# Mixer A's gate products on rounded high and low parts, in the middle of a projection step

## The chip, the cores and the metric

The kernel runs on one core of one Trainium2 chip. The time is the device time of one execution in microseconds (us); of repeated executions the median is taken. TensorE (PE) multiplies, VectorE (DVE), ScalarE (ACT) and GpSimd (POOL) work on vectors, SyncE (SP) and POOL issue the DMAs. Each engine works through its own list of instructions in order and waits for the others at semaphores.

## The reference, cut to what matters

The reference is one step of a one-layer hybrid decoder: 2048 prompt tokens and 8 x 4 sample tokens, width 1024. One input projection gives nine groups of 256 columns; four token mixers (A to D) share them; then come an output projection, a layer norm and a squared-ReLU MLP with a second norm. The change is in mixer A, whose gates `r` and `i` are 64 x 64 products per head:

```python
    xc, new_buf_a = causal_conv(xa, buf_a, conv_a_w)      # width 4, depthwise
    xc = xc + conv_a_b
    # rglru(xc, ...):
    xh = xc.reshape(B, T, N_HEADS, HEAD_DIM)              # 4 heads of 64
    r = jax.nn.sigmoid(jnp.einsum('bthi,hij->bthj', xh, wa).reshape(B, T, W_GROUP) + ba)
    i = jax.nn.sigmoid(jnp.einsum('bthi,hij->bthj', xh, wx).reshape(B, T, W_GROUP) + bx)
    log_a = -RGLRU_C * r * jax.nn.softplus(-lam)
    a = jnp.exp(log_a)
    b = jnp.sqrt(-jnp.expm1(2.0 * log_a)) * (i * xc)
    # h_t = a_t * h_(t-1) + b_t over the tokens
    ya = ha * jax.nn.gelu(ga)
```

## The kernel before, in words

Everything is kept channels first: 128 channels on the partitions, tokens along the row. The 2080 tokens are cut into five blocks of 416 (`BLK`). A product that needs more precision than one rounded (`fp32r`) product gives is made of three: weights and input are each split into a rounded high part (ACT copies to `fp32r`) and the rest (DVE subtracts), and high x high, high x low and low x high are summed in PSUM.

The input projection runs in 88 steps (`P_STEPS`, counted by `j`). A step is one tile of 128 output columns for one block: 24 rounded products (`project`, L869 to L871), into one of three PSUM banks in turn. ACT copies the result out (`put_out`, L1306), and SP stores it to a scratch in DRAM. A step can start only when the result three steps before it has been copied out. Steps 0 to 19 make the four tiles that mixer A needs, block by block; from step 20 on the order is tile by tile, and the mixers run beside the projection.

Mixer A has ten passes, n = 0 to 9: two halves of 128 channels (two heads each) times five blocks. Where the work of a pass stands is set by a table: `A_AT` gives pass n to step 21 + 3n. In the lists of the engines that means:

- POOL loads the pass's two inputs from the scratch (`a_load`), after it has stored the result of the pass two before (`put`, L2482) and that store has ended, since the buffers are shared.
- DVE: `a_conv(n)` makes the convolution (L1802, L1804) at step 21 + 3n, then `a_rest(n - 1)` finishes the pass before: five operations, L1834 to L1849, the scan over the tokens among them.
- PE: `a_gates(n)` (L903) stands ahead of the next step, 22 + 3n: two plain f32 products of `gsel` (for each half of the channels a 128 x 128 matrix with the two heads' 64 x 64 gates on its diagonal) with `a_conv`, into the banks PS 6 and PS 7.
- ACT: `a_act(n)` (L1336) follows `put_out` of step 21 + 3n: two sigmoids out of PSUM (L1343, L1345), then exp, tanh, square root and gelu, with four table loads between them.

The fifth block (n = 4 and 9) holds the sample tokens too, so its convolution and its scan are made of more instructions. Mixer B (`b_mix`, at the steps of `B_AT`, from 37 on) and mixer D (`D_AT`, from 50 on; it uses a third matrix in `gsel`) follow in the same lists.

A table `SPLIT` says at which step the next weight tile is split: ACT's `split_hi` (L1271) stands behind `put_out` of that step, DVE's `split_lo` (L1687) one step later, and waits for it. The entries between steps 21 and 50 are 24, 29, 34, 39, 44 and 49. DVE's place for a step has this order: `a_conv`, `a_rest`, `b_mix`, `d_mix`, `split_lo`.

Before step 20 SP loads the gates into `gsel` with 12 DMAs (L565), and DVE and ACT make the constants of the recurrence (`lam`) from `lru_lambda`.

Of the kernel before, what the change touches and what calls it, by code (L numbers as in the profile page):

```python
# [81 lines left out]
CONST_ALL = 16 * 18  # L82
# [165 lines left out]
def build(nc, x_all, w_all, pvec, lnp, rows2, gates_a, gates_x, poolw, sbh, sbr, masks, ident_d, ck, cv, ptab,  # L248
          st_h, st_a, st_b, st_p, y_out, kv_out, so_out):
    ctx = ExitStack()  # L250
    with ctx:
# [42 lines left out]
        with ExitStack() as e1:  # L294
# [7 lines left out]
            with ExitStack() as f:  # L302
# [14 lines left out]
                d1 = sb("d_sum_a", [P, LASTW + BUFP + DECB * (BUFP + DECT)], F32, f)  # L317
                d2 = sb("d_sum_b", [P, LASTW + BUFP + DECB * (BUFP + DECT)], F32, f)
                d5 = sb("d_mean", [P, BLK], F32, f)
                d6 = sb("d_out", [P, BLK], F32, f)  # L320
# [133 lines left out]
        s_mzero = sem("gate_weights_zeroed")  # L454
        s_axc, s_agp, s_agev, s_aact, s_amade = sem("a_conv_made"), sem("a_gates_done"), sem("a_gates_evacuated"), sem("a_act_done"), sem("ya_made")
# [105 lines left out]
        def _(sp):  # L561
# [71 lines left out]
            for c in range(2):  # L633
                for n, src in enumerate((gates_a, gates_x, poolw)):
                    for h in range(2):
                        const(gsel[HD * h:HD * h + HD, c, n, HD * h:HD * h + HD], src[2 * c + h])
# [201 lines left out]
        def _(pe):  # L838
# [12 lines left out]
            def project(j, amid=(), turned=()):  # L851
# [363 lines left out]
            for j in range(NB * GRP, N_P):  # L1215
                if j - 1 in A_AT:
                    a_gates(A_AT[j - 1])
# [7 lines left out]
                project(j, p_taus(j, 1))  # L1225
# [35 lines left out]
        def _(act):  # L1261
# [75 lines left out]
            def a_act(n):  # L1337
# [13 lines left out]
                act.activation(ag[:, n % 2, :], ag[:, n % 2, :], ACT.Gelu_apprx_tanh).then_inc(s_aact, 1)  # L1351

# [1246 lines left out]
```

## Time and profile before

| | |
|---|---|
| median of 3 runs | 2453.49 us (2453.25 to 2456.35) |
| the profiled execution | 2453.47 us |
| its span, first to last instruction | 2451.9 us |
| PE busy | 2410.5 us, 98% |
| DVE busy | 1587.5 us, 65% |
| ACT busy | 1287.9 us, 53% |
| mean granted clock of TensorE | 0.997 |

The span is what the rows count in; 1.6 us of the profiled execution's time lie around it. In a group of instructions, "idle before" is how long the engine stood still just ahead of them, and the name behind the arrow is what ended that. In a timeline a row is a stretch of equal instructions with its start and its length; matmuls overlap, so the spacing of their starts is what one costs. A table load stands as a row of its own on ACT.

### The profile page before, as it was taken

The numbers are of one execution on the slowest core, as the hardware profiler recorded it, in microseconds if no ns is written. First come the engines' busy times: TensorE is split into PE (matmuls) and PEld (weight loads), VectorE is DVE, ScalarE is ACT, GpSimd is POOL, SyncE is SP. The second block draws the span as 40 slices with busy tenths as digits, with TensorE's granted clock in tenths as the row PEclk, the third lists the DMA queues.
The fourth block names the chain that finished last, engine by engine and source line by source line (L and its number), as shares of the span: only waits on it lengthen the run. The fifth ranks groups of instructions, "written<-read, shape, count | busy, mean of one in ns | idle before, by whom it ended". The sixth has DMA issues, their size and how long they took to land.

```text
span 2451.9 us, 36722 instructions
## 1 busy us (share of the span) xinstructions
PE 2410.5 (98%) x13263; PEld 2330.7 (95%) x13263; DVE 1587.5 (65%) x2234; ACT 1287.9 (53%) x1981; POOL 242.4 (10%) x526
## 2 busy tenths in 40 slices
PE   7999999999999999999999999999999999999998
PEld 7999999999999999999999999999999999999998
DVE  7535662656777787777778777757755665863335
ACT  5466523545656745556555566554445555444432
POOL 0011320200101100111100011000122130000000
PEclk9999999999999999999999999999999999999999
DMA  8434554533444434444443443433566674343332
GB/s 256 152 110 140 165 170 131 168 120 127 160 126 157 130 117 140 131 149 141 122 131 124 130 146 115 133 115 117 173 192 183 203 238 140 117 136 120 112 115 86
DMA packets 141526, 351.64 MB, mean 143 GB/s; under 512 B 20625, under 2 KB 64146, under 8 KB 141218
## 3 DMA queue, kind: packets, MB, share of 16 engines
q1 hardware_dynamic: 128994, 312.88, 40.2%
q0 software_dynamic: 12352, 36.42, 4.7%
q8 instruction: 106, 1.74, 0.3%
q14 instruction: 74, 0.61, 0.1%
HBM read 300.11 MB, written 49.12 MB: 142 GB/s over the span
## 4 chain that ended last, share of the span: by engine, by line
PE 92%; DVE 3%; ACT 2%; issue 1%; DMA 1%; SPq 0%; DVEq 0%; ACTq 0%
PE PS L1133 21%; PE PS L1135 21%; PE PS L1134 21%; PE PS L871 5%; PE PS L869 5%; PE PS L870 5%; PE PS L939 2%; PE PS L961 1%; PE PS L960 1%; PE PS L929 1%; PE PS L1023 1%; PE PS L930 1%; PE PS L1053 1%; PE PS L1011 1%; PE PS L909 1%
## 5 line engine op out<-in xcount | busy, mean ns | idle before, releaser
L1433 ACT ACTIVATE w_hi_lo<-w_raw 128x1024 fp32r<-128x1024 f32 x240 | 253.0, 1054 | 282.8 <-PE PS L1135 276.7
L1133 PE MATMUL PS<-a_hi,w_hi_lo 128*128 128x416 f32 x1080 | 385.0, 356 | 1.9 <-DVE a_lo L2185 1.9
L1135 PE MATMUL PS<-a_hi,w_hi_lo 128*128 128x416 f32 x1080 | 378.9, 351 | 0.0
L1134 PE MATMUL PS<-a_lo,w_hi_lo 128*128 128x416 f32 x1080 | 378.1, 350 | 0.0
L1986 DVE TENSOR_TENSOR w_hi_lo<-w_raw,w_hi_lo 128x1024 fp32r<-128x1024 f32 x240 | 292.7, 1220 | 57.2 <-ACT w_hi_lo L1433 54.9
L1133 PE MATMUL PS<-h_hi,w_hi_lo 128*128 128x416 f32 x824 | 294.3, 357 | 0.0
L1135 PE MATMUL PS<-h_hi,w_hi_lo 128*128 128x416 f32 x824 | 289.8, 352 | 0.0
L1134 PE MATMUL PS<-h_lo,w_hi_lo 128*128 128x416 f32 x824 | 288.9, 351 | 0.0
L2013 DVE TENSOR_TENSOR h_lo<-h_full,h_hi 128x416 fp32r<-128x416 f32 x160 | 94.6, 592 | 224.1 <-ACT h_hi L1448 223.9
L1133 PEld LDWEIGHTS PS<-a_hi,w_hi_lo 128*128 128x128 f32 x1080 | 202.8, 188 | 5.4 <-DVE a_lo L2185 2.8
L1134 PEld LDWEIGHTS PS<-a_lo,w_hi_lo 128*128 128x128 f32 x1080 | 203.3, 188 | 2.1
L1135 PEld LDWEIGHTS PS<-a_hi,w_hi_lo 128*128 128x128 f32 x1080 | 202.4, 187 | 2.3
L1433 ACT ACTIVATE w_hi_lo_c<-w_raw 128x1024 fp32r<-128x1024 f32 x120 | 126.5, 1054 | 132.8 <-PE PS L1135 128.4
L1444 ACT ACTIVATE h_full<-PS 128x416 f32<-128x416 f32 x160 | 82.5, 516 | 200.6 <-PE PS L1135 198.8
L1133 PE MATMUL PS<-a_hi,w_hi_lo_c 128*128 128x416 f32 x520 | 185.2, 356 | 2.2 <-DVE a_lo L2019 2.0
L1942 DVE TENSOR_TENSOR_SCAN n_prompt<-n_prompt 128x512 f32<-128x512 f32 (+3 forms) x160 | 178.9, 1118 | 8.6 <-POOL n_prompt L2508 8.4
L1135 PE MATMUL PS<-a_hi,w_hi_lo_c 128*128 128x416 f32 x520 | 183.2, 352 | 0.0
L1134 PE MATMUL PS<-a_lo,w_hi_lo_c 128*128 128x416 f32 x520 | 182.5, 351 | 0.0
L1986 DVE TENSOR_TENSOR w_hi_lo_c<-w_raw,w_hi_lo_c 128x1024 fp32r<-128x1024 f32 x120 | 146.3, 1220 | 34.1 <-ACT w_hi_lo_c L1433 33.2
L1134 PEld LDWEIGHTS PS<-h_lo,w_hi_lo 128*128 128x128 f32 x824 | 155.6, 189 | 2.1
L1133 PEld LDWEIGHTS PS<-h_hi,w_hi_lo 128*128 128x128 f32 x824 | 155.3, 188 | 2.2 <-issue 0.4
L1135 PEld LDWEIGHTS PS<-h_hi,w_hi_lo 128*128 128x128 f32 x824 | 154.8, 188 | 1.6
(334 smaller groups left out, 5206.4 us busy)
## 6 DMA issues: line engine op xcount, KB each, us to landing
w_raw<-w_all SPq DMA_DIRECT2D x380, 512.0 KB, 3.5
proj_scratch<-stage SPq DMA_DIRECT2D x70, 208.0 KB, 2.0
k_rows<-kv_out SPq DMA_DIRECT2D x80, 128.0 KB, 4.1
v_hi_lo<-v_scratch SPq DMA_DIRECT2D x40, 256.0 KB, 4.3
x_scratch<-x_full SPq DMA_DIRECT2D x20, 416.0 KB, 2.7
x_residual<-x_scratch SPq DMA_DIRECT2D x5, 1664.0 KB, 7.8
pages<-ck SPq DMA_DIRECT2D x64, 128.0 KB, 2.2
pages<-ck POOLq DMA_DIRECT2D x64, 128.0 KB, 2.6
```

Source lines behind the costliest of these rows:

```text
L869: pe.matmul(out, w_h, x_hi(b)[:, k, :], start=(k == 0), stop=False)
L870: pe.matmul(out, w_h, x_lo(b)[:, k, :], start=False, stop=False)
L871: ins = pe.matmul(out, w_l, x_hi(b)[:, k, :], start=False, stop=(k == KT - 1))
L939: ins = pe.transpose(PS[:, 5 + 2 * (t % 2), j * P:(j + 1) * P], sP[:, t % 3, j * P:(j + 1) * P], ident[:, :])
L1133: pe.matmul(out, w_h, mh_[:, k, :], start=(g == 0), stop=False)
L1134: pe.matmul(out, w_h, ml_[:, k, :], start=False, stop=False)
L1135: ins = pe.matmul(out, w_l, mh_[:, k, :], start=False, stop=(g == KT - 1))
L1433: act.activation(halves(w_hi(n)), raw_halves(n), ACT.Copy).then_inc(s_wh, 1)
L1444: act.activation(hf[:, f % 2, :], PS[:, (N_P + n) % 3, 0:BLK], ACT.Relu).then_inc(s_r, 1)
L1942: dve.tensor_tensor_scan(rev(n_t[:, 0:w]), rev(n_t[:, 0:w]), rev(n_t[:, 0:w]), n_t[:, w:w + 1], ALU.mult, ALU.bypass).then_inc(s_scan2, 1)
L1986: dve.tensor_tensor(halves(w_lo(n)), raw_halves(n), halves(w_hi(n)).bitcast(F32), ALU.subtract).then_inc(s_wl, 1)
L2013: dve.tensor_tensor(hl[:, i, :], hf[:, f % 2, :], hh[:, i, :].bitcast(F32), ALU.subtract).then_inc(s_hl, 1)
```

## The change

The gates' products become rounded ones. One product takes the input of one head, its high part on 64 partitions and its low part on the other 64, against a weight matrix that holds the head's gates twice, above each other; its 128 output rows are that head's 64 rows of `r` and 64 rows of `i`. So a bank holds one head's two gates, where it held one gate of two heads. The sum of two such products, with the high and with the low part of the weights, is the whole product. That makes four rounded products for each pass in place of two f32 ones.

What this takes: 20 DMAs into `gsel` in place of 12; ACT and DVE split the gates once (`gate_w_hi`, `gate_w_lo`); in each pass ACT copies the convolution's two halves to the high part (`a_conv_hi`) and DVE makes the low one (`a_conv_lo`); the sigmoids are four on 64 partitions each, two of them with partitions swapped, for which two rows of `lru_bx` are copied. `a_gates` moves from ahead of a step into its middle, behind 12 of its 24 products. `a_conv_hi(n)` stands on ACT ahead of `put_out` of step 21 + 3n, and `a_conv_lo(n)` on DVE behind `a_rest(n - 1)`. The new tiles share the space of mixer D's sums, so mixer D's first pass waits for the last gates.

```diff
-            def project(j, amid=(), turned=()):
+            def project(j, amid=(), turned=(), gates=None):
...
                     if k == KT // 2:
                         if j in V_AT_STEP:
                             turn_v(V_AT_STEP[j])
+                        if gates is not None:
+                            a_gates(gates)
...
             def a_gates(n):
 
-                pe.wait_ge(s_axc, n + 1)
-                for what in (0, 1):
+                if n == 0:
+                    pe.wait_ge(s_gwl, 1)
+                pe.wait_ge(s_gxl, n + 1)
+                for h in (0, 1):
                     if n:
-                        pe.wait_ge(s_agev, 2 * n - 1 + what)
-                    pe.matmul(PS[:, 6 + what, 0:BLK], gsel[:, n // NB, what, :], axc[:, n % 2, :], start=True, stop=True).then_inc(s_agp, 1)
+                        pe.wait_ge(s_agev, 2 * n - 1 + h)
+                    out, x = PS[:, 6 + h, 0:BLK], conv_hl[:, h, :]
+                    pe.matmul(out, gate_w[:, 0, n // NB, h, :], x, start=True, stop=False)
+                    pe.matmul(out, gate_w[:, 1, n // NB, h, :], x, start=False, stop=True).then_inc(s_agp, 1)
...
             for j in range(NB * GRP, N_P):
-                if j - 1 in A_AT:
-                    a_gates(A_AT[j - 1])
...
-                project(j, p_taus(j, 1))
+                project(j, p_taus(j, 1), gates=A_AT.get(j - 1))
...
                 act.wait_ge(s_agp, 2 * n + 1)
-                act.activation(ar[:, :], PS[:, 6, 0:BLK], ACT.Sigmoid, bias=pv[:, c, PBA:PBA + 1]).then_inc(s_agev, 1)
+                act.activation(ar[0:HD, :], PS[0:HD, 6, 0:BLK], ACT.Sigmoid, bias=pv[0:HD, c, PBA:PBA + 1])
+                act.activation(ai[0:HD, :], PS[HD:P, 6, 0:BLK], ACT.Sigmoid, bias=lam[HD:P, c, 6:7]).then_inc(s_agev, 1)
                 act.wait_ge(s_agp, 2 * n + 2)
-                act.activation(ai[:, :], PS[:, 7, 0:BLK], ACT.Sigmoid, bias=pv[:, c, PBX:PBX + 1]).then_inc(s_agev, 1)
-                wait_apart(act, s_agev, 2 * n + 1)
+                act.activation(ar[HD:P, :], PS[HD:P, 7, 0:BLK], ACT.Sigmoid, bias=pv[HD:P, c, PBA:PBA + 1])
+                act.activation(ai[HD:P, :], PS[0:HD, 7, 0:BLK], ACT.Sigmoid, bias=lam[0:HD, c, 6:7]).then_inc(s_agev, 1)
+                wait_apart(act, s_agev, 2 * n + 2)
...
+            def gate_w_hi():
+
+                for m in s_t1st:
+                    act.wait_ge(m, 16 * NB)
+                act.activation(gate_w[:, 0, :, :, :], gsel[:, :, 0:2, :], ACT.Copy).then_inc(s_gwh, 1)
+
+            def a_conv_hi(n):
+
+                act.wait_ge(s_axc, n + 1)
+                if n:
+                    act.wait_ge(s_agp, 2 * n)
+                for h, rows in enumerate((slice(0, HD), slice(HD, P))):
+                    act.activation(conv_hl[rows, h, :], axc[rows, n % 2, :], ACT.Copy).then_inc(s_gxh, 1)
...
                     act.wait_ge(s_lam, 3)
+                    gate_w_hi()
+                if j in A_AT:
+                    a_conv_hi(A_AT[j])
...
+            def gate_w_lo():
+
+                dve.wait_ge(s_gwh, 1)
+                dve.tensor_tensor(gate_w[:, 1, :, :, :], gsel[:, :, 0:2, :], gate_w[:, 0, :, :, :].bitcast(F32), ALU.subtract).then_inc(s_gwl, 1)
+
+            def a_conv_lo(n):
+
+                dve.wait_ge(s_gxh, 2 * n + 2)
+                for h, rows, low in ((0, slice(0, HD), slice(HD, P)), (1, slice(HD, P), slice(0, HD))):
+                    ins = dve.tensor_tensor(conv_hl[low, h, :], axc[rows, n % 2, :], conv_hl[rows, h, :].bitcast(F32), ALU.subtract)
+                ins.then_inc(s_gxl, 1)
...
                 if j - 3 in A_AT:
                     a_rest(A_AT[j - 3])
+                if j in A_AT:
+                    if A_AT[j] == 0:
+                        gate_w_lo()
+                    a_conv_lo(A_AT[j])
                 if j in B_AT:
                     b_mix(B_AT[j])
```

How the lists of the engines read at three places. On DVE, at steps 27 and 30 (pass 2's convolution is followed by the end of pass 1, then comes pass 3's convolution), before:

```order
L1802 TENSOR_SCALAR a_conv<-a_x,pv 128x416 [waits a_gates_done,a_inputs_in0]
L1804 SCALAR_TENSOR_TENSOR a_conv<-a_x,pv,a_conv 128x416 [waits dve_own] x3
L1834 TENSOR_TENSOR a_i<-a_i,a_conv 128x416 [waits dve_own,a_act_done]
L1835 SCALAR_TENSOR_TENSOR a_root<-a_t,a_root 128x416
L1836 TENSOR_TENSOR a_root<-a_root,a_i 128x416 [waits dve_own]
L1838 SCALAR_TENSOR_TENSOR a_state<-a_t,a_state,a_root 128x416 [waits dve_own]
L1849 TENSOR_TENSOR a_gate<-a_state,a_gate 128x416 [waits dve_own]
L1802 TENSOR_SCALAR a_conv<-a_x,pv 128x416 [waits a_gates_done,a_inputs_in1]
```

and now:

```order
L1835 TENSOR_SCALAR a_conv<-a_x,pv 128x416 [waits a_gates_done,a_inputs_in0]
L1837 SCALAR_TENSOR_TENSOR a_conv<-a_x,pv,a_conv 128x416 [waits dve_own] x3
L1879 TENSOR_TENSOR a_i<-a_i,a_conv 128x416 [waits dve_own,a_act_done]
L1880 SCALAR_TENSOR_TENSOR a_root<-a_t,a_root 128x416
L1881 TENSOR_TENSOR a_root<-a_root,a_i 128x416 [waits dve_own]
L1883 SCALAR_TENSOR_TENSOR a_state<-a_t,a_state,a_root 128x416 [waits dve_own]
L1894 TENSOR_TENSOR a_gate<-a_state,a_gate 128x416 [waits dve_own]
L1870 TENSOR_TENSOR a_conv_hi_lo<-a_conv,a_conv_hi_lo 64x416 [waits a_conv_hi_made]
L1870 TENSOR_TENSOR a_conv_hi_lo<-a_conv,a_conv_hi_lo 64x416
L1835 TENSOR_SCALAR a_conv<-a_x,pv 128x416 [waits a_gates_done,a_inputs_in1]
```

What PE waits for stood ahead of the five operations of `a_rest` and now stands behind them; the first of the five waits for ACT's gelu (`a_act_done`).

On DVE at steps 33 to 36 (pass 3's last operation, then a weight tile's low part, then pass 5's convolution and pass 4's end), before:

```order
L1849 TENSOR_TENSOR a_gate<-a_state,a_gate 128x416 [waits dve_own]
L1687 TENSOR_TENSOR w_hi_lo<-w_raw,w_hi_lo 128x2x512 [waits w_hi_made]
L1820 MEMSET a_x 128x3 [waits a_inputs_in1]
L1802 TENSOR_SCALAR a_conv<-a_x,pv 128x416 [waits dve_own,a_gates_done]
L1804 SCALAR_TENSOR_TENSOR a_conv<-a_x,pv,a_conv 128x416 [waits dve_own] x3
L1834 TENSOR_TENSOR a_i<-a_i,a_conv 128x416 [waits dve_own,a_act_done]
```

and now:

```order
L1894 TENSOR_TENSOR a_gate<-a_state,a_gate 128x416 [waits dve_own]
L1870 TENSOR_TENSOR a_conv_hi_lo<-a_conv,a_conv_hi_lo 64x416 [waits a_conv_hi_made]
L1870 TENSOR_TENSOR a_conv_hi_lo<-a_conv,a_conv_hi_lo 64x416
L1718 TENSOR_TENSOR w_hi_lo<-w_raw,w_hi_lo 128x2x512 [waits w_hi_made]
L1853 MEMSET a_x 128x3 [waits a_inputs_in1]
L1835 TENSOR_SCALAR a_conv<-a_x,pv 128x416 [waits dve_own,a_gates_done]
L1837 SCALAR_TENSOR_TENSOR a_conv<-a_x,pv,a_conv 128x416 [waits dve_own] x3
L1879 TENSOR_TENSOR a_i<-a_i,a_conv 128x416 [waits dve_own,a_act_done]
```

The weight tile's low part stands ahead of pass 5's convolution in both; it is the one of the six that stands between a pass's `a_act` and the `a_rest` of the same pass with a convolution behind it.

On ACT, pass 0 (`stage` is `put_out` of step 21), before:

```order
L1306 ACTIVATE stage<-PS 128x416 [waits stage_stored1,proj_step_done]
L1343 ACT_TABLE_LOAD
L1343 ACTIVATE a_r<-PS,pv 128x416 [waits a_gates_done]
L1345 ACTIVATE a_i<-PS,pv 128x416 [waits a_gates_done]
L1347 ACT_TABLE_LOAD [waits a_gates_evacuated]
L1347 ACTIVATE a_t<-a_r,lam 128x416
```

and now:

```order
L1379 ACTIVATE a_conv_hi_lo<-a_conv 64x416 [waits a_conv_made]
L1379 ACTIVATE a_conv_hi_lo<-a_conv 64x416
L1318 ACTIVATE stage<-PS 128x416 [waits stage_stored1,proj_step_done]
L1355 ACT_TABLE_LOAD
L1355 ACTIVATE a_r<-PS,pv 64x416 [waits a_gates_done]
L1356 ACTIVATE a_i<-PS,lam 64x416
L1358 ACTIVATE a_r<-PS,pv 64x416 [waits a_gates_done]
L1359 ACTIVATE a_i<-PS,lam 64x416
L1361 ACT_TABLE_LOAD [waits a_gates_evacuated]
L1361 ACTIVATE a_t<-a_r,lam 128x416
```

Two copies have come ahead of `put_out`, and two sigmoids more stand between the gates and the rest of the pass.

## Rows read from the trace of the kernel before

**Rows 1.** The page's busy times of the engines over the span.

```profile
PE 2410.5 (98%) x13263; PEld 2330.7 (95%) x13263; DVE 1587.5 (65%) x2234; ACT 1287.9 (53%) x1981; POOL 242.4 (10%) x526
```

**Rows 2.** The chain that ended last (start, us, what): first and last gates.

```profile
135.66 1.40 PE PS L909 x4
...
270.72 1.40 PE PS L909 x4
```

**Rows 3.** PE in order of time (start, length), around pass 0's gates.

```profile
135.31 0.35 PE L871 MATMUL PS<-x_early,w_hi_lo 128*128 128x416 f32 x1
135.50 1.56 PE L909 MATMUL PS<-a_conv,gsel 128*128 128x416 f32 x4
...
137.09 0.35 PE L870 MATMUL PS<-x_late,w_hi_lo 128*128 128x416 f32 x1
```

**Rows 4.** ACT in order of time: pass 2, and the copies of two later steps.

```profile
166.35 1.28 ACT L1343 ACT_TABLE_LOAD   x1 [0.23 <-PE PS L909]
167.65 0.61 ACT L1343 ACTIVATE a_r<-PS,pv 128x416 f32<-128x416 f32 x1
168.15 0.60 ACT L1345 ACTIVATE a_i<-PS,pv 128x416 f32<-128x416 f32 x1
...
174.47 0.55 ACT L1351 ACTIVATE a_gate<-a_gate 128x416 f32<-128x416 f32 x1
...
290.97 0.52 ACT L1306 ACTIVATE stage<-PS 128x416 f32<-128x416 f32 x1 [3.90 <-PE PS L871]
295.47 0.52 ACT L1306 ACTIVATE stage<-PS 128x416 f32<-128x416 f32 x1 [3.99 <-PE PS L871]
```

**Rows 5.** DVE in order of time: end of pass 2, pass 4's convolution, end of pass 3.

```profile
175.05 0.59 DVE L1834 TENSOR_TENSOR a_i<-a_i,a_conv 128x416 f32<-128x416 f32 x1 [1.86 <-ACT a_gate L1351]
...
178.14 0.59 DVE L1849 TENSOR_TENSOR a_gate<-a_state,a_gate 128x416 f32<-128x416 f32 x1
178.65 1.22 DVE L1687 TENSOR_TENSOR w_hi_lo<-w_raw,w_hi_lo 128x1024 fp32r<-128x1024 f32 x1
186.85 0.69 DVE L1802 TENSOR_SCALAR a_conv<-a_x,pv 128x384 f32<-128x384 f32 x2 [6.99 <-DMA a_x<-st_a]
...
190.46 0.59 DVE L1834 TENSOR_TENSOR a_i<-a_i,a_conv 128x416 f32<-128x416 f32 x1
```

**Rows 6.** Instructions by line and shape (xcount | busy us, mean ns | idle before).

```profile
L1921 DVE TENSOR_TENSOR q_hi_lo<-q_rows,q_hi_lo 64x512 fp32r<-64x512 f32 x16 | 11.1, 691 | 36.1 <-ACT q_hi_lo L1365 35.7
...
L1409 ACT ACTIVATE y_low_part<-PS 64x512 f32<-64x512 f32 x16 | 9.6, 597 | 0.4
```

**Rows 7.** ACT in order of time: the end of pass 4's gelu.

```profile
204.39 0.55 ACT L1351 ACTIVATE a_gate<-a_gate 128x416 f32<-128x416 f32 x1
```

**Rows 8.** DVE in order of time, behind it.

```profile
206.33 1.23 DVE L1687 TENSOR_TENSOR w_hi_lo<-w_raw,w_hi_lo 128x1024 fp32r<-128x1024 f32 x1 [12.20 <-ACT w_hi_lo L1271]
...
210.60 0.59 DVE L1834 TENSOR_TENSOR a_i<-a_i,a_conv 128x416 f32<-128x416 f32 x1
...
214.81 0.58 DVE L1849 TENSOR_TENSOR a_gate<-a_state,a_gate 128x416 f32<-128x416 f32 x1
```

**Rows 9.** PE in order of time: the first product behind two waits.

```profile
413.26 0.38 PE L929 MATMUL PS<-k_hi_lo,q_hi_lo 128*128 128x256 f32 x1 [2.05 <-ACT n_prompt L1392]
...
539.23 0.46 PE L1133 MATMUL PS<-a_hi,w_hi_lo 128*128 128x416 f32 x1 [1.46 <-DVE a_lo L2185]
```

**Rows 10.** A stretch of 2 us: engines' busy times, then the granted clock (0.57).

```profile
414.00:416.00 2.00, 2.00 (x8) 1.93 (x7) 0.78 (x2) 0.65 (x2) 0.58 (x3) 0.57 0.74 224
```

**Rows 11.** Issues of the gates' DMAs: ns min/median/max, first and last start.

```profile
L565 SPq DMA_DIRECT2D gsel<-gates_x x4: 596/597/1447, 110.7 to 115.1; - x4
L565 SPq DMA_DIRECT2D gsel<-poolw x4: 597/597/606, 111.9 to 117.3; - x4
```

**Rows 12.** DVE in order of time: its last instruction before it needs ACT.

```profile
121.32 0.16 DVE L1771 TENSOR_TENSOR lam<-pv,lam 128x2 f32<-128x2 f32 x1
```

**Rows 13.** ACT in order of time: its first instruction on the constants.

```profile
127.17 1.28 ACT L1605 ACT_TABLE_LOAD   x1
```

More of the change, by code:

```diff
@@ L81 @@
 XFB = NB * KT // 2
-CONST_ALL = 16 * 18
+CONST_ALL = 16 * 26
 def ext_of(tile, halo):
@@ L316, in build @@
                 dx = sb("d_x", [P, 2, LASTW + BUFP + DECB * (BUFP + DECT)], F32, f)
[L317 to L320, printed above, removed]
+                with ExitStack() as g:
+                    d1 = sb("d_sum_a", [P, LASTW + BUFP + DECB * (BUFP + DECT)], F32, g)
+                    d2 = sb("d_sum_b", [P, LASTW + BUFP + DECB * (BUFP + DECT)], F32, g)
+                    d5 = sb("d_mean", [P, BLK], F32, g)
+                    d6 = sb("d_out", [P, BLK], F32, g)
+                with ExitStack() as g:
+                    gate_w = sb("gate_w_hi_lo", [P, 2, 2, 2, P], F32R, g)
+                    conv_hl = sb("a_conv_hi_lo", [P, 2, BLK], F32R, g)
         with ExitStack() as e1:
@@ L454, in build @@
         s_mzero = sem("gate_weights_zeroed")
+        s_gwh, s_gwl, s_gxh, s_gxl = sem("gate_w_hi_made"), sem("gate_w_lo_made"), sem("a_conv_hi_made"), sem("a_conv_lo_made")
         s_axc, s_agp, s_agev, s_aact, s_amade = sem("a_conv_made"), sem("a_gates_done"), sem("a_gates_evacuated"), sem("a_act_done"), sem("ya_made")
@@ L633, in _ @@
             for c in range(2):
-                for n, src in enumerate((gates_a, gates_x, poolw)):
-                    for h in range(2):
-                        const(gsel[HD * h:HD * h + HD, c, n, HD * h:HD * h + HD], src[2 * c + h])
+                for h in range(2):
+                    for rows in (slice(0, HD), slice(HD, P)):
+                        for n, src in enumerate((gates_a, gates_x)):
+                            col = HD * (n ^ h)
+                            const(gsel[rows, c, h, col:col + HD], src[2 * c + h])
+                    const(gsel[HD * h:HD * h + HD, c, 2, HD * h:HD * h + HD], poolw[2 * c + h])
             assert n_const[0] == CONST_ALL
@@ L1783, in _ @@
             op(dve.scalar_tensor_tensor(out=L(5), in0=L(4), scalar=0.0, in1=L(5), op0=ALU.max, op1=ALU.add))
+            own.up(dve.tensor_copy(lam[0:HD, :, 6], pv[HD:P, :, PBX]))
+            own.up(dve.tensor_copy(lam[HD:P, :, 6], pv[0:HD, :, PBX]))
             own.up(dve.tensor_scalar(L(2), L(5), -RC, None, ALU.mult))
@@ L1892, in d_mix @@
                 every, low, high = slice(0, P), slice(0, HD), slice(HD, P)
+                if n == 0:
+                    dve.wait_ge(s_agp, 4 * NB)
                 wider(d1, x, 1, every)
```

## The prediction

> **What bounds the kernel now.** I read the page's busy times first: PE is busy for 98% of the span, DVE for 65%, ACT for 53% [rows 1]. Then the chain of waits: through the stretch of the ten passes it is PE alone, the f32 gates among it [rows 2]. So whatever PE does there costs its own length, and every wait added to PE does too. Then the timelines of PE, ACT and DVE through single passes, since the change also moves what PE waits for.
>
> **What PE saves.** From the product before pass 0's gates to the second one behind them 1.78 us pass [rows 3]; products without gates lie 0.19 us apart, so two of them would take 0.37 and the gates cost 1.40. The first and last gates lie 135.06 us apart [rows 2], nine times 15.01; three steps take 3 x 4.50 [rows 4], which leaves 1.50 for each. I take 1.45. Four rounded products at 0.19 cost 0.75 (bounds 0.75 and 1.4: they have the form of the products around them, but no row shows them). Saved: 0.70 each, 7.0 us in all, if PE never waits.
>
> **The loop that the change closes.** Before, PE's gates of pass n + 1 needed only the convolution, and the rest of pass n ran beside PE. Now they need `a_conv_lo(n + 1)`, which stands on DVE behind `a_rest(n)`, which waits for ACT's gelu of pass n, which comes behind the gates of pass n. So gates wait for gates. One turn, from rows:
> - Gates to table load: two products (0.19 + 0.35), about 0.06 for the semaphore: 0.60.
> - Table load to the end of gelu: 166.35 to 175.02, 8.67 [rows 4]. The two added sigmoids come at the spacing of the present two, 0.50: halving the partitions saves nothing, since 64x512 takes 0.60 on ACT [rows 6]. Exp now waits for the last sigmoid, about 0.06. Together 9.74.
> - DVE: 0.03, then the end of the pass from 175.05 to 178.73, 3.68. The next instruction starts 0.51 behind the last one's start [rows 5]. Two subtractions on 64 partitions: 64x512 takes 0.69 [rows 6] and 128x416 0.59 [rows 5], so 0.59 each, together 1.02 behind the end of the pass. Sum 4.73.
> - DVE's end to PE's first product: 0.15 (bounds 0.05 and 0.3; the first product behind a wait is 0.1 longer [rows 9]).
>
> The turn is 15.22 us; PE alone needs 3 x 4.50 + 0.75 = 14.25. PE waits about 0.97 in a usual interval, and the 0.70 saved there is gone. The copies `a_conv_hi` (0.5 each) aren't in the turn: ACT has them behind the gelu, where two `put_out` at 0.5 and at times a weight tile at 1.05 stand too; that ends by 13.4 us behind the gates, before DVE wants it at 14.0.
>
> **The long turn, pass 4 to 5.** At step 35 DVE stands in `split_lo`, waiting for ACT's `split_hi` of step 34, which ACT reaches only after pass 4's gelu. Then come that split, pass 5's convolution and the longer end of pass 4 (eight short scans). Before, it took from 204.94 [rows 7] to 215.39, with the split at 206.33 and the end of the pass starting at 210.60 [rows 8]: 10.45 us, and PE didn't wait, because pass 5's convolution was ready at 210.5. Now `a_conv_lo(5)` stands behind all of it: 0.60 + 9.74 + 10.45 + 1.02 + 0.15 = 21.96, 7.71 more than PE needs.
>
> **Two turns with late inputs, 3 to 4 and 8 to 9.** The convolution of a fifth block waited for its state by DMA until 186.85, and the end of the pass behind it started at 190.46, 11.73 behind the end of the pass two before [rows 5]. In the new order that end lies 1.17 ahead of the gates, so `a_rest` starts 10.56 behind them where gelu allows 10.37: 15.41.
>
> **The clock.** After a wait of 2.05 us, shortly behind a short one, the granted clock fell to 0.57 (mostly the 1.2 GHz level) for two stretches of 2 us, of which one stands in [rows 9, 10]; behind a wait of 1.46 it did not fall. So the wait of 7.7 should bring it down, and waits of 1 us should not. Cost by these rows: 4 x 0.43 = 1.7 us. It falls into turn 5 to 6, where PE then needs 14.25 + 1.7 = 15.95, more than the loop's 15.22. The Trainium skill ("TensorE: Matmul & The Clock Gate", Part 1) has PE at the lower level after an idle time and at the higher once it is kept busy; the trace agrees, with the numbers above.
>
> A rule that speaks harder against this change: the Trainium skill ("ScalarE: Activation LUTs", What ACT_TABLE_LOAD costs) gives about 2.66 us to every switch of tables, load and drain together. By it four switches would make the turn some 5.5 us longer. The trace disagrees: the sigmoid starts 1.30 behind the load's start [rows 4], so the sum goes by 1.30.
>
> **The first gates.** They stand 2.25 us (12 products) later in their step: 135.66 + 2.25 = 137.91. Are they ready? Eight more DMAs at 0.60 each put the constants back by 4.8 us, or 5.7 with one long issue of 1.45 [rows 11]. DVE's part ended at 121.48 [rows 12]; 4.8 to 5.7 later is 126.3 to 127.2, and ACT first wanted it at 127.17 [rows 13]. SP's next stores and weight loads slip too, but those slots have steps to spare. Splitting the gates and the first convolution takes ACT and DVE to about 137.3, so PE waits for neither (at worst 0.5 to 1.0 us).
>
> **The sum.** Intervals between gates: five usual ones 5 x 15.22 = 76.10, two with late inputs 30.82, the long one 21.96, the one behind it 15.95; total 144.83 (before 135.06). The last gates begin at 137.91 + 144.83 = 282.74 and step 49 ends 0.75 + 2.25 later, at 285.74. Before, it ended at 270.72 + 1.45 + 4.50 = 276.67. Difference +9.1 us. Behind it pass 9 ends about 4 us later relative to PE; mixer D's second product, which is behind it on DVE, keeps some 1.3 us, and mixer D's first pass finds the last gates long done. From then on PE bounds the kernel as before, so the shift stays.
>
> Against the profiled execution (2453.47, span 2451.9 and 1.6 around it) that is 2462.5; its time is the median's to 0.02 us, so the median should be 2462.5.
>
> **Rivals.**
> - *No loop, the saving stays (faster).* One mechanism: `a_conv_lo(n + 1)` comes in time. It decides at a turn of 14.25 us, so ACT and DVE together would have to be 1 us quicker than their rows, and the long turn would have to vanish. Then PE saves 7.0: 2446.5. For it speaks that PE hides nearly everything else in this trace; against it, that each link is the same instruction as in the rows and stands in a fixed order. If only the long turn remains, the sum is -7.0 + 7.7 + 1.7 = +2.4, 2455.9.
> - *The usual turns bind, the long one is shorter.* Without it +9.1 - 6.7 - 0.7 = +1.7, 2455.2. Against it: the three instructions between are in the list, and DVE did wait 12.20 us for that split [rows 8].
> - *The clock falls often.* If waits of 1 us brought it down each time, PE would need about 15.95 in each of the seven other intervals, where the loop has 15.22 or 15.41: 5 x 0.73 + 2 x 0.54 = 4.7 us more, 2467.2; with slower gates and restarts up to 2470. For it: the wait of 2.05 that did it; against: 1.46 did not [rows 9].
> - *The first gates late*: up to +1, 2463.5. This lies in the forecast's own range.
>
> **How the numbers follow.** Forecast 75%: its own range comes from 0.2 us per turn in eight turns (1.6), 0.5 in the long one, 0 to 2.5 for the clock, 1 at the start, and the later stage that may give back up to 2: 2459.5 to 2466.5. No loop 5%; only the long turn or only the usual ones 9%; the clock 11%. Range for 8 in 10: 2457.5 to 2467.5. A measurement of this kernel can tell about 0.2%, 4.9 us: faster means under 2448.6, slower over 2458.4. Faster 0.06, same 0.11, slower 0.83.
>
> **What would show it.** PE: about 1 us idle ahead of the second to last gates, ended by DVE's line of `a_conv_lo`, and one wait near 7.7 in step 37. Gates 15.2 apart in the usual turns, 22 in the long one. Four sigmoids 0.50 apart. Gates' products 0.19 apart. A granted clock below 1 behind the long wait and nowhere else before step 50. ACT free of waits for `a_conv`. The prediction is wrong if PE has no such waits, if the usual turn is under 14.6 or over 16, or if PE waits elsewhere, for a PSUM bank above all: `put_out` of the step with the gates ends only 1.3 us before its bank is wanted.

## The result, and the profile after

The changed kernel takes 2475.47 us (median of 4 runs, 2474.40 to 2478.14) against 2454.35 (4 runs, 2453.25 to 2456.35): 1.0087 of the time before, 95% interval 1.0074 to 1.0100. Slower, as forecast, but by 21 us where the forecast had 9, and outside its range (2457.5 to 2467.5). All times here are medians of executions that agree; one execution of run 5, 9117.37 us at a mean granted clock of 0.252, is left out of its median.

The page's busy times, where [rows 1] stood before: PE is busy 1.7 us longer in a span 21.4 us longer.

```profile
span 2473.3 us, 36806 instructions
...
PE 2412.2 (98%) x13263; PEld 2335.0 (94%) x13263; DVE 1600.1 (65%) x2257; ACT 1310.7 (53%) x2022; POOL 239.4 (10%) x526
```

What PE waited for between 100 and 440 us (in all, times, longest), the row that the change adds:

```profile
PE PS L922 <- DVE a_conv_hi_lo L1870: 18.2, 8, 5.6
```

A turn is the spacing of two passes' first gate products (PE L922). The ten starts are 139.68, 154.31, 170.09, 185.89, 204.26, 227.19, 243.33, 259.12, 274.91 and 292.76. PE at pass 2 (a usual wait), at pass 4 (state input), 5 (the long turn) and 9 (state input again):

```profile
170.09 0.46 PE L922 MATMUL PS<-a_conv_hi_lo,gate_w_hi_lo 128*128 128x416 f32 x1 [1.16 <-DVE a_conv_hi_lo L1870]
...
204.26 0.71 PE L922 MATMUL PS<-a_conv_hi_lo,gate_w_hi_lo 128*128 128x416 f32 x1 [3.83 <-DVE a_conv_hi_lo L1870]
204.77 0.55 PE L923 MATMUL PS<-a_conv_hi_lo,gate_w_hi_lo 128*128 128x416 f32 x1
205.12 0.55 PE L922 MATMUL PS<-a_conv_hi_lo,gate_w_hi_lo 128*128 128x416 f32 x1
...
227.19 0.71 PE L922 MATMUL PS<-a_conv_hi_lo,gate_w_hi_lo 128*128 128x416 f32 x1 [5.59 <-DVE a_conv_hi_lo L1870]
...
292.76 0.72 PE L922 MATMUL PS<-a_conv_hi_lo,gate_w_hi_lo 128*128 128x416 f32 x1 [3.23 <-DVE a_conv_hi_lo L1870]
```

Behind a usual gate wait the granted clock stayed at 1.00 (184 to 190 us, around the wait of 1.20). Behind the three long ones it read 0.50 to 0.60, mostly the 1.2 GHz level, and the products start 0.35 apart in place of 0.19.

ACT through pass 2, where [rows 4] stood:

```profile
170.82 1.28 ACT L1355 ACT_TABLE_LOAD   x1 [3.35 <-PE PS L923]
172.12 0.60 ACT L1355 ACTIVATE a_r<-PS,pv 64x416 f32<-64x416 f32 x1
172.73 0.61 ACT L1356 ACTIVATE a_i<-PS,lam 64x416 f32<-64x416 f32 x1
173.37 0.60 ACT L1358 ACTIVATE a_r<-PS,pv 64x416 f32<-64x416 f32 x1
...
180.35 0.55 ACT L1365 ACTIVATE a_gate<-a_gate 128x416 f32<-128x416 f32 x1
```

The four sigmoids stand 0.61 to 0.64 apart, not 0.50. DVE behind it, as in [rows 5], with pass 4's convolution, and DVE in the long turn, as in [rows 8]:

```profile
180.94 0.59 DVE L1879 TENSOR_TENSOR a_i<-a_i,a_conv 128x416 f32<-128x416 f32 x1 [3.09 <-ACT a_gate L1365]
...
184.02 0.59 DVE L1894 TENSOR_TENSOR a_gate<-a_state,a_gate 128x416 f32<-128x416 f32 x1
184.65 1.19 DVE L1870 TENSOR_TENSOR a_conv_hi_lo<-a_conv,a_conv_hi_lo 64x416 fp32r<-64x416 f32 x2
...
195.36 0.69 DVE L1835 TENSOR_SCALAR a_conv<-a_x,pv 128x384 f32<-128x384 f32 x2 [8.27 <-DMA a_x<-st_a]
...
216.86 1.23 DVE L1718 TENSOR_TENSOR w_hi_lo<-w_raw,w_hi_lo 128x1024 fp32r<-128x1024 f32 x1 [12.66 <-ACT w_hi_lo L1283]
...
225.95 1.19 DVE L1870 TENSOR_TENSOR a_conv_hi_lo<-a_conv,a_conv_hi_lo 64x416 fp32r<-64x416 f32 x2
```

The two subtractions start 0.63 behind the multiply and take 1.19 together. The state's DMA, issued by POOL, with SP's issue of a weight tile near it (start, length). Before:

```profile
179.89 0.33 SPq L572 DMA_DIRECT2D w_raw<-w_all  x1
...
183.49 0.89 POOL L2450 DMA_DIRECT2D a_x<-st_a  x1
```

and after:

```profile
187.12 0.33 SPq L577 DMA_DIRECT2D w_raw<-w_all  x1
...
189.36 0.89 POOL L2501 DMA_DIRECT2D a_x<-st_a  x1
```

Before, the convolution began 3.4 us behind that issue [rows 5]; now it begins 6.0 behind it. The weight tile's issue stands 2.2 us ahead of the state's, where it was 3.6.

### The profile page after: what moved, and what is told of

It is laid out like the page before. It is cut to its first block, busy times and chain, and to the rows that moved or that the text cites. A ratio compares the mean times of both kernels' runs of the same rounds, so it can differ in the third digit from the quotient of the medians.

```text
span 2473.3 us, 36806 instructions
## 1 busy us (share of the span) xinstructions
PE 2412.2 (98%) x13263; PEld 2335.0 (94%) x13263; DVE 1600.1 (65%) x2257; ACT 1310.7 (53%) x2022; POOL 239.4 (10%) x526
## 4 chain that ended last, share of the span: by engine, by line
PE 85%; issue 6%; DVE 4%; ACT 2%; DMA 2%; POOL 1%; SPq 1%; DVEq 0%; ACTq 0%; POOLq 0%
PE PS L1147 21%; PE PS L1149 21%; PE PS L1148 21%; PE PS L881 3%; PE PS L879 3%; PE PS L880 3%; PE PS L953 2%; PE PS L975 1%; PE PS L974 1%; PE PS L943 1%; PE PS L1037 1%; PE PS L944 1%; PE PS L1067 1%; PE PS L1025 1%; DMA mixed_scratch<-a_gate 1%
```

## The experiments

All are edits of the changed kernel; its 2475.47 us is what each is compared with, unless said otherwise. A ratio is always to the kernel before, run beside it; its medians there are 2453.92 to 2454.32 us. Turns are read as above.

**1. PE doesn't wait for the convolution** (its products read other tiles, so the result lacks the gates; tile 8 is split a step later).

```diff
-                pe.wait_ge(s_gxl, n + 1)
...
-                    out, x = PS[:, 6 + h, 0:BLK], conv_hl[:, h, :]
+                    out, x = PS[:, 6 + h, 0:BLK], x_hi(0)[:, h, :]
...
-                    act.wait_ge(s_agp, 2 * n)
+                    act.wait_ge(s_gxl, n)
```

> The changed kernel, but the gates' products read two resident tiles of the rounded input in place of the split convolution, so PE waits for no convolution (the gates' values are left out of the result); the convolution is split as before, and the weight split of step 34 stands at step 35. Everything that PE, ACT and DVE do is still there. Theory (PE's own work got cheaper by 0.7 us a pass, and all of the loss is waits in the loop gates, ACT, end of the pass, a_conv_lo, gates): no PE wait in steps 22 to 49, products of the gates 0.19 apart, intervals of 14.25 to 14.3, time 7 us under the kernel before, about 2447. Rival (the added work itself, the mid-step place or SBUF traffic costs PE something): intervals over 14.6, or waits for a PSUM bank, time at or over 2454.

Measured: 2449.57 us, ratio to before 0.9982 (0.9972 to 0.9991). The turns are 14.3 to 14.4 where PE isn't held, 14.5 on the mean of nine, and the gates' products are 0.19 apart. PE's only new wait in the stretch:

```profile
PE PS L879 <- ACT stage L1317: 0.8, 2, 0.4
```

That is 2.6 us above the 2447 expected, and under the rival's 2454. So the loss is the wait on DVE, with what the clock lost behind it: without it the kernel is 25.9 us faster, of which the later split alone (run 3) gives at most 7.7. Part of the saving of the cheaper products is there too: mixer D's first product, at 285.6 before, is at 280.8, 4.8 of the 7.0 expected.

**2. The low part ahead of the end of the pass before.**

```diff
-                if j - 3 in A_AT:
-                    a_rest(A_AT[j - 3])
                 if j in A_AT:
...
                     a_conv_lo(A_AT[j])
+                if j - 3 in A_AT:
+                    a_rest(A_AT[j - 3])
```

> The changed kernel with a_conv_lo(n) ahead of a_rest(n - 1) on DVE, nothing else. Theory: the end of the pass leaves the loop, but a_conv_hi still stands on ACT behind gelu, and a_rest is later, so the store and the load of the next input are too; a usual turn is then held by the loop lo, a_rest (3.7), store and load (6.5), convolution (2.7), hi (1.1), lo (1.2): about 15.3 in place of 15.8; the long turn 18.8 in place of 22.9. Time 4 to 9 us under the changed kernel, 2466 to 2471. Rival (the order on DVE is all of it): every turn 14.25, time about 2450.

Measured: 2472.4 us, ratio 1.0075 (1.0055 to 1.0095); turns 14.39, 14.35, 16.34, 19.09, 20.47, 16.73, 16.26, 16.51, 17.98. Only 3 us gained, above the expected range: the order on DVE is not enough. I took the rest for a second loop through the store and the load of the inputs; run 11 tests that.

**3. Tile 8 split at step 35 and not 34.**

```diff
-SPLIT = {16: 4, 17: 5, 24: 6, 29: 7, 34: 8,
+SPLIT = {16: 4, 17: 5, 24: 6, 29: 7, 35: 8,
```

> The changed kernel with the weight split of step 34 at step 35, so that DVE's part stands behind a_conv_lo(5) and not between pass 4's gelu and its end. Theory: only the turn 4 to 5 changes, from 22.9 to 16.9 us (0.73 + 10.08 + 0.04 + 4.80 + 1.23 + 0.05), and the clock stays up behind it; 6 to 7 us less than the changed kernel, 2468 to 2469.5. Rival (the long turn was pass 4's longer end and late inputs, not the split): under 2 us less.

Measured: 2467.82 us, ratio 1.0054 (1.0038 to 1.0071). The turn 4 to 5 falls from 22.93 to 17.31, 5.6 us, where 6.0 was expected; so the split in DVE's list is what made most of this turn long. The time falls by 7.7, 0.2 below the expected range. That this is also the 7.71 by which the prediction had the long turn over what PE needs is chance: the turn is still 3 us longer than PE needs, and mixer D's first product moves by 6.2, of which 1.6 is an earlier start of the first gates.

**4. Tiles 7 and 10 split three steps later**, which moves their loads away from the state inputs.

```diff
-24: 6, 29: 7, 34: 8, 39: 9, 44: 10, 49: 11,
+24: 6, 32: 7, 34: 8, 39: 9, 47: 10, 49: 11,
```

> The changed kernel with the weight splits of steps 29 and 44 at 32 and 47, so that the 512 KB weight loads they release no longer run beside the loads of the sample state for passes 4 and 9. Theory (contention: in the changed kernel both are issued within 2.5 us, before they were 3.6 us apart): the state lands 3.3 us after its issue in place of 5 to 6, the turns 3 to 4 and 8 to 9 take about 15.9 in place of 18.4 and 17.9, the clock stays up behind them; 5 to 7 us less than the changed kernel, 2468.5 to 2470.5. Rival (the small packets of the state land late for another reason): the two turns stay within 0.5 us and so does the time.

Measured: 2469.63 us, ratio 1.0062 (1.0046 to 1.0079). Turn 3 to 4 falls from 18.37 to 16.82, turn 8 to 9 from 17.85 to the usual 15.79. The state's DMA lands 4.4 and 3.2 us behind its issue, where it took 6.0 and 5.8. So the load of a weight tile beside the state's transfer (and its split in the way, which this edit moves too) is a large part of what made these turns long; in the turn 3 to 4, expected at 15.9, something is left. There the wait of 2.26 still brought the clock down:

```profile
200.74 0.71 PE L922 MATMUL PS<-a_conv_hi_lo,gate_w_hi_lo 128*128 128x416 f32 x1 [2.26 <-DVE a_conv_hi_lo L1870]
201.25 0.55 PE L923 MATMUL PS<-a_conv_hi_lo,gate_w_hi_lo 128*128 128x416 f32 x1
201.60 0.55 PE L922 MATMUL PS<-a_conv_hi_lo,gate_w_hi_lo 128*128 128x416 f32 x1
```

**5. The gates ahead of the step again.**

```diff
-                        if gates is not None:
-                            a_gates(gates)
...
+                if j - 1 in A_AT:
+                    a_gates(A_AT[j - 1])
```

> The changed kernel with the gates' products ahead of the step, where they stood before, not in its middle. Theory (the loop sets when the gates run, not their place): turns as in the changed kernel, 15.8 in the usual ones, each wait about as long; behind the last gates a whole step follows in place of half, so 2.2 us more, 2476 to 2479. Rival (the middle of the step makes everything late): the turns get shorter and the time falls by 2 us or more, under 2473.5.

Measured: 2476.2 us (3 runs, 2474.96 to 2480.20), ratio 1.0094 (1.0076 to 1.0112); PE waits 19.4 us for the low part. The place in the middle of the step isn't what costs. Whether it hides a little can't be told: the two kernels' runs overlap.

**6. Two sigmoids on 128 partitions.**

```diff
-                act.activation(ar[0:HD, :], PS[0:HD, 6, 0:BLK], ACT.Sigmoid, bias=pv[0:HD, c, PBA:PBA + 1])
-                act.activation(ai[0:HD, :], PS[HD:P, 6, 0:BLK], ACT.Sigmoid, bias=lam[HD:P, c, 6:7]).then_inc(s_agev, 1)
+                act.activation(ar[:, :], PS[:, 6, 0:BLK], ACT.Sigmoid, bias=pv[:, c, PBA:PBA + 1]).then_inc(s_agev, 1)
...
+                act.activation(ai[:, :], PS[:, 7, 0:BLK], ACT.Sigmoid, bias=pv[:, c, PBX:PBX + 1]).then_inc(s_agev, 1)
```

> The changed kernel with two sigmoids on 128 partitions in place of four on 64, straight from the two banks (so the halves of the two gates are exchanged and the result is not the gates' any more; everything else as it is). Theory (the loop through ACT, and halves that cost as much as wholes and don't overlap): the table load to gelu takes 8.8 in place of 10.1, every turn is 1.25 shorter, the usual ones 14.55; time 8 to 11 us less than the changed kernel, 2464.5 to 2467.5. Rival (something else on DVE or by DMA sets the usual turn): usual turns over 15.2.

Measured: 2469.96 us, ratio 1.0063 (1.0045 to 1.0081). The usual turns are 14.3 to 14.5, as PE alone needs, so the four-sigmoid form costs all of what PE waits in them. The time missed by 2.5 us: the turns with a state input stayed at 18.34 and 17.94 and didn't get 1.25 shorter, and the turn 5 to 6, where PE has no wait, is 16.57. ACT:

```profile
169.97 0.61 ACT L1355 ACTIVATE a_r<-PS,pv 128x416 f32<-128x416 f32 x1
170.47 0.60 ACT L1357 ACTIVATE a_i<-PS,pv 128x416 f32<-128x416 f32 x1
```

**7. Four sigmoids, the two on the low 64 partitions first, then the two on the high ones**, each read and written on the same partitions.

```diff
+                act.activation(ar[0:HD, :], PS[0:HD, 6, 0:BLK], ACT.Sigmoid, bias=pv[0:HD, c, PBA:PBA + 1])
+                act.activation(ai[0:HD, :], PS[0:HD, 7, 0:BLK], ACT.Sigmoid, bias=pv[0:HD, c, PBX:PBX + 1])
+                act.activation(ar[HD:P, :], PS[HD:P, 6, 0:BLK], ACT.Sigmoid, bias=pv[HD:P, c, PBA:PBA + 1]).then_inc(s_agev, 1)
+                act.activation(ai[HD:P, :], PS[HD:P, 7, 0:BLK], ACT.Sigmoid, bias=pv[HD:P, c, PBX:PBX + 1]).then_inc(s_agev, 1)
```

> The changed kernel with its four sigmoids in another order: two from partitions 0 to 63 to partitions 0 to 63, then two from 64 to 127 to 64 to 127 (each takes its input from the same partitions, so part of the gates is exchanged). It asks why sigmoids on 64 partitions start 0.62 apart where those on 128 start 0.50 apart. If an instruction does not overlap the one before it when its partition range differs: starts 0.50, 0.62, 0.50 apart and turns of about 15.55. If it is that they have 64 partitions: 0.62 throughout and 15.8.

One execution, 2479.92 us. ACT:

```profile
174.65 0.60 ACT L1356 ACTIVATE a_r<-PS,pv 64x416 f32<-64x416 f32 x1
175.16 0.59 ACT L1357 ACTIVATE a_i<-PS,pv 64x416 f32<-64x416 f32 x1
175.76 0.60 ACT L1358 ACTIVATE a_r<-PS,pv 64x416 f32<-64x416 f32 x1
176.27 0.59 ACT L1359 ACTIVATE a_i<-PS,pv 64x416 f32<-64x416 f32 x1
```

0.51 within a range of partitions, 0.60 where it changes, 0.51 again. On ACT, with these shapes, an instruction starts under the end of the one before it only where both work on the same partitions. The turn did not get shorter (15.8 to 15.9): from table load to the end of gelu it is 9.83 us in place of 10.08, but ACT here waits for both banks, and its table load starts 1.12 us behind the first gate product in place of 0.73.

**8. DVE makes the high part too, both parts right behind the convolution**; splits at 32, 35 and 47.

```diff
-                    a_conv_hi(A_AT[j])
...
-                dve.wait_ge(s_gxh, 2 * n + 2)
+                if n:
+                    dve.wait_ge(s_agp, 2 * n)
+                for h, rows in enumerate((slice(0, HD), slice(HD, P))):
+                    own.up(dve.tensor_copy(conv_hl[rows, h, :], axc[rows, n % 2, :]))
+                own.sync()
```

with the order on DVE of run 2.

> The same rounded gates in the middle of the step, but DVE makes both parts of the convolution's split itself, right behind the convolution and ahead of the end of the pass before, so ACT is out of it; the weight splits of steps 29, 34 and 44 stand at 32, 35 and 47. Theory (no loop through gelu any more; what is left is the round of store, load, convolution and split over two passes, about 26 us where PE needs 28.5): no PE wait from the second gates on, intervals 14.25 to 14.4, time 5 to 7 us under the kernel before, 2447 to 2449. Rival (two more DVE operations a pass make the end of the pass and the next input late): waits ahead of the gates of 0.5 us or more, time over 2452.

Measured: 2462.32 us, ratio 1.0032 (1.0020 to 1.0044), a miss by 13 us. The first three turns are 14.4, then 14.97, 16.30, 17.84, 15.54, 15.38 and 17.08. DVE waits for pass 4's state until 190.19, and pass 3's end stands behind it; ACT then has to wait for that end before pass 4's first sigmoid, the same happens a pass later, and PE waits for a bank that ACT copies out late. DVE, then ACT, then PE:

```profile
190.19 0.69 DVE L1833 TENSOR_SCALAR a_conv<-a_x,pv 128x384 f32<-128x384 f32 x2 [8.50 <-DMA a_x<-st_a]
...
196.24 0.59 DVE L1881 TENSOR_TENSOR a_i<-a_i,a_conv 128x416 f32<-128x416 f32 x1
...
199.32 0.59 DVE L1896 TENSOR_TENSOR a_gate<-a_state,a_gate 128x416 f32<-128x416 f32 x1
```

```profile
199.95 0.60 ACT L1355 ACTIVATE a_r<-PS,pv 64x416 f32<-64x416 f32 x1 [1.68 <-DVE a_gate L1896]
```

```profile
226.71 0.43 PE L879 MATMUL PS<-x_early,w_hi_lo 128*128 128x416 f32 x1 [1.79 <-ACT stage L1318]
```

**9. The convolution's inputs loaded early.** `a_load` waited as a whole for the store of the pass two before, though only `a_gate`'s buffer needs that. Here `a_x` waits for the convolution two passes before, and is issued ahead of the store; `a_gate` has a semaphore of its own.

```diff
-                    pool.wait_ge(s_mst[0], 16 * (n - 1))
+                    pool.wait_ge(s_axc, n - 1)
...
+                if j + 2 in A_AT and A_AT[j + 2]:
+                    a_load(A_AT[j + 2])
                 if j - 4 in A_AT:
                     put(0, A_AT[j - 4], ag[:, A_AT[j - 4] % 2, :], s_amade, 0)
...
                 if j + 2 in A_AT and A_AT[j + 2]:
-                    a_load(A_AT[j + 2])
+                    a_load_gate(A_AT[j + 2])
```

> Theory (state inputs land late because a_load as a whole waits for the store of the pass two before): the convolution's inputs are issued ahead of that store here, and only the gate input behind it, so the two turns with a state input fall from 18.37 and 17.85 us to the usual 15.8, and the clock stays up behind them: -5.0 for the two turns, about -1 for the end; 2469 to 2471. The long turn stays at 22 to 23. Rival (the turn is long because DVE's convolution and scan of a fifth block are made of more instructions, whatever the input does): the turns stay above 17.3 and the time above 2473.

Measured: 2467.86 us, ratio 1.0056 (1.0041 to 1.0072). The state's DMA is issued at 172.39, and the turns with a state input are 15.79 and 15.79; the gain is 7.6 us, more than expected. In this profile mixer D's first product is 7.4 us earlier: 4.6 from those two turns, 1.3 behind the last gates, where the wait is 1.15 and the clock stays up, 1.2 because this run's first gates are earlier, 0.4 in the long turn, less 0.1 in the turn behind it. The state now lands 2.8 to 3.0 us behind its issue, and DVE never waits for it.

```profile
172.39 0.89 POOL L2500 DMA_DIRECT2D a_x<-st_a  x1
```

```profile
286.60 0.46 PE L923 MATMUL PS<-a_conv_hi_lo,gate_w_hi_lo 128*128 128x416 f32 x1 [1.15 <-DVE a_conv_hi_lo L1871]
```

The rival, a fifth block's longer list of instructions, is refuted: that list is as long as before.

**10. Runs 8 and 9 together.**

> The high part made by DVE, both parts ahead of the end of the pass before, weight tiles 7, 8 and 10 split one to three steps later (as in the kernel without the loop on PE's side), and the convolution's inputs loaded early. Theory: late state inputs were all that kept that kernel from its 14.4 us turns; all nine turns then lie at 14.3 to 15.1, the first product of mixer D at 281 to 283, and the time is 2449 to 2453. Rival (the end of a pass standing behind the next convolution and its two parts holds a_act and with it put_out): turns 4 to 5 and 5 to 6 stay at 16 to 18 us, PE waits for put_out for 2 us or more, and the time is 2456 to 2460.

Measured: 2449.67 us (11 runs, 2447.56 to 2453.01), ratio 0.9982 (0.9973 to 0.9991). It is faster than both kernels. The one edit against run 8 is worth 12.7 us. All nine turns lie between 14.29 and 14.41, and PE waits for nothing of mixer A. PE at pass 4's gates, and the first product of mixer D:

```profile
194.71 0.35 PE L923 MATMUL PS<-a_conv_hi_lo,gate_w_hi_lo 128*128 128x416 f32 x1
194.89 0.35 PE L924 MATMUL PS<-a_conv_hi_lo,gate_w_hi_lo 128*128 128x416 f32 x1
...
278.59 0.86 PE L931 MATMUL PS<-d_mean,gsel 128*128 128x416 f32 x2
```

Here PE is 7.0 us ahead of before, as much as the products save; at the end 5.1 us of span are left, and 4.4 between the medians. The waits for `n_prompt`, `k_hi_lo` and `s_prompt` grew by 1.4 us in all over the whole span.

**11. Runs 2 and 9 together.**

> The low part ahead of the end of the pass before (as in the run with the two exchanged), with the convolution's inputs loaded early. Theory: that run's turns of 16.3 to 16.7 us came from a second loop, end of pass, store, load, convolution, ACT's high part, and the early loads cut it. What is left is ACT: its high part stands behind a_act and two put_out (about 14.2 us behind the gates, 15.2 where a weight tile's split stands between, steps 29 and 44). So five to six turns at 14.4, two at about 15.3, the long one at 17 to 18; 2455 to 2459. Rival (ACT's place for the high part alone makes the 16.4): turns stay above 16, and the time above 2463.

Measured: 2468.06 us, ratio 1.0055 (1.0040 to 1.0071). A miss by 9 us, and the rival's time. The early loads shorten the two turns with a state input (19.09 and 17.98 in run 2), but not the usual ones: the store and the load are not what bound those. Turns: 14.38, 14.35, 16.10, 15.57, 20.46, 17.07, 15.13, 16.52, 15.56. ACT shows the real loop:

```profile
162.51 0.55 ACT L1366 ACTIVATE a_gate<-a_gate 128x416 f32<-128x416 f32 x1
162.96 0.91 ACT L1319 ACTIVATE stage<-PS 128x416 f32<-128x416 f32 x2
163.76 1.11 ACT L1380 ACTIVATE a_conv_hi_lo<-a_conv 64x416 fp32r<-64x416 f32 x2
...
167.20 1.28 ACT L1356 ACT_TABLE_LOAD   x1 [1.78 <-PE PS L924]
169.84 0.60 ACT L1356 ACTIVATE a_r<-PS,pv 64x416 f32<-64x416 f32 x1 [1.36 <-DVE a_gate L1895]
...
186.35 0.61 ACT L1356 ACTIVATE a_r<-PS,pv 64x416 f32<-64x416 f32 x1 [1.68 <-DVE a_gate L1895]
...
201.93 0.60 ACT L1356 ACTIVATE a_r<-PS,pv 64x416 f32<-64x416 f32 x1 [1.67 <-DVE a_gate L1895]
```

Pass n's high part is made behind gelu of pass n - 1; the low part waits for it; the end of pass n - 1 now stands behind the low part; and the first sigmoid of pass n waits for that end, because `a_r` and `a_i` are single buffers. From first sigmoid to first sigmoid that is 15.6 us, or 16.5 with a weight tile's split between. Run 2 has it too. What its ACT waited for between 130 and 300 us (in all, times, longest):

```profile
ACT a_r L1355 <- DVE a_gate L1894: 14.1, 9, 2.4
```

Making the high part on DVE breaks this loop: run 12 differs from this one in nothing else, and is 12.8 us faster.

**12. Run 10 with the splits at 29, 34 and 44 again.**

> As the kernel at 2449.67 us, but the weight tiles are split at steps 29, 34 and 44 again. Theory: tile 8's low part stands between gelu of pass 4 and the convolution of pass 5, which is ready only at about 18.3 us behind pass 4's gates; the turn 4 to 5 grows by 3.9 us and the clock falls behind it (up to 1.7), the other turns stay at 14.4: 2453.5 to 2455.5. Rival (early inputs suffice whatever the splits' places): below 2451.

Measured: 2455.31 us (11 runs), ratio 1.0002 (0.9993 to 1.0011). Turn 4 to 5 is 18.47 (18.3 expected), the one behind it 17.19, the others 14.3 to 14.4. PE has no wait in the one behind it, so its extra 2.8 us is the clock's, where up to 1.7 was expected. The three splits' places are worth 5.6 us against run 10, and the time is the same as before the change. PE's busy time and clock around the wait of 3.90 (2 us a row: length, busy, granted clock, DMA share, GB/s):

```profile
216.00:218.00 2.00, 0.93 (x3) 0.58 0.29 109
218.00:220.00 2.00, 2.00 (x7) 0.50 0.04 8
220.00:222.00 2.00, 2.00 (x7) 0.50 0.00 0
222.00:224.00 2.00, 2.00 (x9) 0.72 0.30 107
```

## Why the prediction was wrong

The mechanism was right: gates wait for gates through DVE's list, PE's saving is lost in it, and pass 4 to 5 is the worst turn. Its sizes were wrong, and one term, the two turns with a state input, makes nearly half of the miss. In the two profiles mixer D's first product moves from 285.6 to 306.2, 20.6 us. The sum had 9.1. The 11.6 between are, term by term (0.2 more fell into the turn 5 to 6):

- **State inputs, +5.4, the largest.** The forecast had 15.41 for each of the turns 3 to 4 and 8 to 9; they took 18.37 and 17.85. The step that failed: "The convolution of a fifth block waited for its state by DMA until 186.85, and the end of the pass behind it started at 190.46, 11.73 behind the end of the pass two before." I carried that distance over as if it were fixed. It is issue plus transfer. The issue did keep its distance: it stands 4.8 us behind the end of pass 2 in both profiles. The transfer did not: the state landed 3.3 to 3.4 us behind its issue before, and 5.8 to 6.0 now, since a weight tile's issue stands 2.2 us ahead of it. In all six profiles with that spacing (the change, runs 1, 3, 5, 6, 7) it takes 4.5 to 6.1; in the eight others 2.7 to 4.4. Run 4 (loads moved apart) takes 3.6 of the 5.4 away, run 9 (issued early) 4.6; what is left there is the usual turn's 15.79 against the 15.41 said.
- **First gates, +1.8.** Said 137.91, seen 139.68. About 1.0 of it is the program's first DMA, which ends at other times in every profile (6.7 to 8.0 us long over these runs), not part of the change. The rest is a wait of 0.84 that I had priced at up to 1.0 and then left at zero in the sum.
- **Usual turns, +1.7.** Said 15.22, seen 15.79 in four of five: sigmoids 0.62 and not 0.50 apart (+0.34), the subtractions likewise (+0.20), gates to table load 0.73 and not 0.60 (+0.13), less 0.10 for a shorter restart of PE. The step that failed: "The two added sigmoids come at the spacing of the present two, 0.50: halving the partitions saves nothing". That halving saves nothing is true; the spacing isn't, as runs 6 and 7 show. The fifth, turn 0 to 1, took 14.63: ACT had its table load done before the late first gates.
- **Clock at the end, +1.5.** The wait ahead of pass 9's gates was 3.23, not about 1, and the clock fell behind it, which the sum had only once; against run 9, where it stays up, that costs 1.3. It fell behind the wait of 3.83 at pass 4 too, against the sign "nowhere else before step 50"; PE then reached pass 5's gates later, so the wait there was 5.59 and not 7.7. In the turn 5 to 6 the forecast was near (15.95, seen 16.14): PE has no wait in it, so its clock cost 1.8 where 1.7 was put. That one price would do for each fall is not so: 1.3, 1.8, and 2.8 in run 12, by how many products ran 0.35 apart (7, 9 and 16 spacings).
- **The long turn, +1.0.** Said 21.96, seen 22.93. The clock was already down when pass 4's gates ran, so gates to table load took 1.14; the rest is the two half-partition terms above. Run 3 confirms that the split stood in the way.

Right were the saving of the products (0.19 apart in runs 1 and 10), the table loads, DVE's 12 us wait for the split, the turns without loops at 14.3 to 14.4 (14.25 said), and that the waits of 1.2 leave the clock up. The rival "no loop" was priced at 2446.5; runs 1 and 10, where there is none, take 2449.6 and 2449.7. Run 10 has the whole lead of 7.0 us at mixer D's first product and 5.1 us of span at the end; 1.4 of the difference is the waits named there, 0.5 stays open, and so does why its median is only 4.4 ahead. In the changed kernel, 0.8 of the 21.4 us of span come behind mixer D's first product, and are not explained either.

The Trainium skill ("ScalarE: Activation LUTs", What ACT_TABLE_LOAD costs) says that back-to-back ACTIVATEs overlap by about 93 ns. Here that holds in runs 6 and 7 on the same partitions (0.60 long, 0.50 to 0.51 apart) and not where the range changes (0.60 apart).

## What to carry to other kernels

When a change makes the bound engine wait for something new, write down the whole cycle from that wait back to itself, with every instruction queued between and every single buffer that it passes; removing one loop can leave the next, 15.6 or 16.5 us long where PE needs 14.4. A DMA that another engine waits for should not be placed by its old distance: find what issues it, what that waits for, and what else is moving then; here splitting one load by what each half really needs was worth 7.6 us in the changed kernel and 12.7 once the loop through ACT was gone. Here instructions on half the partitions cost as much as whole ones, and a little more when the halves alternate.

## What the hardware showed

- Alternating partition ranges cost about 0.1 us an instruction on ACT (0.60 to 0.62 against 0.50 to 0.51), and the two 64-row subtractions on DVE end 1.19 behind the first one's start, with each 0.59 long, so no overlap there either.
- The clock's fall doesn't follow the length of a wait alone: behind 3.83, 5.59 and 3.23 us products came at the lower level at once; behind 3.56 in run 2 it fell only 1.4 us after the restart. In run 5 it fell behind 2.06 and 2.44 and not behind 2.19, and behind 2.46 (pass 9, run 2) it stayed at 1.00:

```profile
288.00:290.00 2.00, 0.46 (x3) 1.00 0.61 230
290.00:292.00 2.00, 1.09 (x6) 1.00 0.28 107
```

  What decides it is left open.
- A small transfer can be late though little is moving. The DMA engines' busy tenths in the changed kernel from 183 to 196 us, 40 slices of 0.325 us:

```profile
DMA  8000000008910009726379999999900000000000
```

  They stop near 192.4, and DVE starts on the state at 195.36. What those last 3 us are was not tried.
